# Feed-forward of a two-block model: where VectorE squares a unit's sums, and where the high and low copies of the features are made

## The reference, cut to what matters

```python
for l in range(DEPTH):                                   # DEPTH = 2
    ...
    x = layer_norm(DEEPNORM_ALPHA * x + h, ln1_g[l], ln1_b[l]).astype(dtype)
    f = jnp.square(jax.nn.relu(jnp.einsum('btd,df->btf', x, w_ff1[l])))
    h = jnp.einsum('btf,fd->btd', f, w_ff2[l])
    x = layer_norm(DEEPNORM_ALPHA * x + h, ln2_g[l], ln2_b[l]).astype(dtype)
```

## Time and profile before

| | |
|---|---|
| median of 3 runs | 3498.74 us (3498.04 to 3498.79) |
| the profiled execution | 3498.18 us |
| its span, first instruction to last | 3496.4 us |
| PE busy (matmuls) | 3399.0 us, 97% |
| TensorE's wait in unit 4 for low copies of features | 12.9 us in 8 waits |
| DVE busy | 2225.9 us, 64% |
| ACT busy | 1640.3 us, 47% |
| DMA queue of SP | 56.9% of 16 engines' span |

### The profile page before, as it was taken

One profiled execution on the slowest core, in us unless ns is written; L12 is line 12 of the kernel. 1 busy time (PEld: TensorE's weight loads), 2 busy tenths in 40 slices (PEclk: granted clock), 3 DMA queues, 4 the chain that ended last, 5 costly groups with the idle time before them and its releaser, 6 DMA issues.

```text
span 3496.4 us, 42741 instructions
## 1 busy us (share of the span) xinstructions
PE 3399.0 (97%) x15987; PEld 2831.0 (81%) x15987; DVE 2225.9 (64%) x2582; ACT 1640.3 (47%) x2086; POOL 383.8 (11%) x454
## 2 busy tenths in 40 slices
PE   9999999999999998989999999999999989999999
PEld 7788778888887787878788888878888879888877
DVE  6986565555555688865665555666446776655654
ACT  4444444444444346443544444444445643355553
POOL 0034001010101000340101010100000132000100
PEclk9999999999999999999999999999999999999999
DMA  7655566666666665456666666666666701665634
GB/s 240 178 145 163 181 207 202 197 204 198 203 198 196 185 199 156 139 156 193 241 204 201 201 200 203 200 186 207 186 180 172 209 14 51 188 188 172 177 120 162
DMA packets 326492, 629.63 MB, mean 180 GB/s; under 512 B 25497, under 2 KB 29593, under 8 KB 324651
## 3 DMA queue, kind: packets, MB, share of 16 engines
q1 hardware_dynamic: 313104, 595.93, 56.9%
q0 software_dynamic: 13216, 31.28, 2.8%
HBM read 612.44 MB, written 2.10 MB: 176 GB/s over the span
## 4 chain that ended last, share of the span: by engine, by line
PE 83%; DVE 9%; ACT 3%; DMA 2%; issue 1%; POOL 1%; SPq 1%; DVEq 0%; ACTq 0%; POOLq 0%
PE ps_unit L278 25%; PE ps_unit L280 25%; PE ps_unit L279 25%; DVE sb_w_lo L262 3%; PE ps_mix L2724 2%; DVE sb_conv_y L1252 2%; DMA sb_raw<-in_w_ff_dram 2%; PE ps_mix L1326 1%; ACT sb_w_hi L255 1%; DMA sb_raw<-in_w_in_dram 1%; SPq L875 1%; PE ps_mix L707 0%; PE ps_mix L306 0%; DVE sb_x L437 0%; PE ps_mix L3121 0%
## 5 line engine op out<-in xcount | busy, mean ns | idle before, releaser
L262 DVE TENSOR_TENSOR sb_w_lo<-sb_raw,sb_w_hi 128x1024 fp32r<-128x1024 f32 x1120 | 1381.6, 1248 | 998.1 <-ACT sb_w_hi L255 992.9
L255 ACT ACTIVATE sb_w_hi<-sb_raw 128x1024 fp32r<-128x1024 f32 x1120 | 1173.3, 1059 | 1341.8 <-DMA sb_raw<-in_w_ff_dram 629.7
L278 PE MATMUL ps_unit<-sb_w_hi,sb_a_hi 128*128 128x512 f32 x3456 | 1363.8, 395 | 16.5 <-DVE sb_a_lo L749 11.2
L280 PE MATMUL ps_unit<-sb_w_hi,sb_a_lo 128*128 128x512 f32 x3456 | 1350.4, 391 | 0.0
L279 PE MATMUL ps_unit<-sb_w_lo,sb_a_hi 128*128 128x512 f32 x3456 | 1349.9, 391 | 0.0
L278 PEld LDWEIGHTS ps_unit<-sb_w_hi,sb_a_hi 128*128 128x128 f32 x3456 | 652.0, 189 | 154.9 <-DVE sb_a_lo L749 12.9
L280 PEld LDWEIGHTS ps_unit<-sb_w_hi,sb_a_lo 128*128 128x128 f32 x3456 | 651.5, 189 | 137.7
L279 PEld LDWEIGHTS ps_unit<-sb_w_lo,sb_a_hi 128*128 128x128 f32 x3456 | 652.2, 189 | 132.1
L278 PE MATMUL ps_unit<-sb_w_hi,sb_f_hi 128*128 128x512 f32 x1024 | 401.6, 392 | 12.9 <-DVE sb_f_lo L1005 12.9
L279 PE MATMUL ps_unit<-sb_w_lo,sb_f_hi 128*128 128x512 f32 x1024 | 399.8, 390 | 0.0
L280 PE MATMUL ps_unit<-sb_w_hi,sb_f_lo 128*128 128x512 f32 x1024 | 399.6, 390 | 0.0
(11 more groups left out here) (464 smaller groups left out, 2003.2 us busy)
## 6 DMA issues: line engine op xcount, KB each, us to landing
sb_raw<-in_w_ff_dram SPq DMA_DIRECT2D x512, 512.0 KB, 3.9
sb_raw<-in_w_in_dram SPq DMA_DIRECT2D x224, 512.0 KB, 3.7
sb_raw<-in_e_w_in_dram SPq DMA_DIRECT2D x112, 512.0 KB, 3.6
sb_raw<-in_o_w_in_dram SPq DMA_DIRECT2D x112, 512.0 KB, 3.9
sb_raw<-in_w_out_dram SPq DMA_DIRECT2D x64, 512.0 KB, 4.7
sb_raw<-in_e_w_out_dram SPq DMA_DIRECT2D x32, 512.0 KB, 4.6
sb_raw<-in_o_w_out_dram SPq DMA_DIRECT2D x32, 512.0 KB, 3.7
sb_f_in<-sb_f_out POOLq DMA_DIRECT2D x256, 32.0 KB, 2.0
```

The costliest lines, as they stand in the source:

```text
L255: k.nc.scalar.activation(k.w_hi[:, j], k.raw[:, j], ACT.Copy).then_inc(k.hi_ready, 1)
L262: k.nc.vector.tensor_tensor(k.w_lo[:, j], k.raw[:, j], k.w_hi[:, j].bitcast(F32), ALU.subtract).then_inc(k.lo_ready, 1)
L278: k.nc.tensor.matmul(acc, hi[:, kt, tokens], w_hi, start=kt == 0, stop=False)
L280: last = k.nc.tensor.matmul(acc, lo[:, kt, tokens], w_hi, start=False, stop=kt == KT - 1)
```

## The change

It touches only the loops of the feed-forward part, in the loops of units 1 to 4. VectorE's squaring stood behind split 3 and now stands behind split 1. ACT's high copies stood behind split 4 and now stand behind split 1. VectorE's low copies stood behind split 4 and now stand behind split 2. No instruction is added or taken away, and no wait.

```diff
@@ act_feed_forward, group(): for j in range(AHEAD, AHEAD + 4)
                 act_split(act, k, b0, u * BLOCKS + j)
                 if between:
                     between(u, j - AHEAD)
+                if 1 <= u <= 4 and j == AHEAD + 1:
+                    act.wait_ge(k.relu2_ready, n + u)
+                    for t in range(TT):
+                        last = k.nc.scalar.activation(feature_tokens(k.f_hi, u - 1, t), feature_rows(k, u - 1, t), ACT.Copy)
+                    last.then_inc(k.f_hi_ready, 1)
@@ act_feed_forward, group(): for j in range(AHEAD + 4, AHEAD + 8)
-                if 1 <= u <= 4 and j == AHEAD + 4:
-                    act.wait_ge(k.relu2_ready, n + u)
...
-                    last.then_inc(k.f_hi_ready, 1)
@@ dve_feed_forward, group(): for j in range(AHEAD, AHEAD + 4)
                 dve_split(dve, k, b0, u * BLOCKS + j)
                 if between:
                     between(u, j - AHEAD)
-            if 1 <= u <= 4:
-                dve.wait_ge(k.f_moved_sp[(u - 1) % 2], q * (32 * SP_SQUARES) + (2 * layer * FF_GROUPS + (u + 1) // 2) * 16 * SP_SQUARES)
...
+                if 1 <= u <= 4 and j == AHEAD + 1:
+                    dve.wait_ge(k.f_moved_sp[(u - 1) % 2], q * (32 * SP_SQUARES) + (2 * layer * FF_GROUPS + (u + 1) // 2) * 16 * SP_SQUARES)
+                    dve.wait_ge(k.f_moved_pool[(u - 1) % 2], q * (32 * (SQUARES - SP_SQUARES)) + (2 * layer * FF_GROUPS + (u + 1) // 2) * 16 * (SQUARES - SP_SQUARES))
+                    dve.wait_ge(k.f_kept, n + u)
+                    sums = k.f_in[:, (u - 1) % 2, :]
+                    k.nc.vector.scalar_tensor_tensor(k.f_out[:, (u - 1) % 2, :], sums, 0.0, sums, ALU.max, ALU.mult)\
+                        .then_inc(k.relu2_ready, 1)
+                if 1 <= u <= 4 and j == AHEAD + 2:
+                    dve.wait_ge(k.f_hi_ready, n + u)
+                    for t in range(TT):
+                        last = k.nc.vector.tensor_tensor(feature_tokens(k.f_lo, u - 1, t), feature_rows(k, u - 1, t),
+                                                         feature_tokens(k.f_hi, u - 1, t).bitcast(F32), ALU.subtract)
+                    last.then_inc(k.f_lo_ready, 1)
@@ dve_feed_forward, group(): for j in range(AHEAD + 4, AHEAD + 8)
-                if 1 <= u <= 4 and j == AHEAD + 4:
-                    dve.wait_ge(k.f_hi_ready, n + u)
...
-                    last.then_inc(k.f_lo_ready, 1)
```

More of the change, by code:

```diff
@@ L934, in group @@
                     between(u, j - AHEAD)
-                if 1 <= u <= 4 and j == AHEAD + 4:
-                    act.wait_ge(k.relu2_ready, n + u)
-                    for t in range(TT):
-                        last = k.nc.scalar.activation(feature_tokens(k.f_hi, u - 1, t), feature_rows(k, u - 1, t), ACT.Copy)
-                    last.then_inc(k.f_hi_ready, 1)
             if u < 4:
@@ L1001, in group @@
                     between(u, j - AHEAD)
-                if 1 <= u <= 4 and j == AHEAD + 4:
-                    dve.wait_ge(k.f_hi_ready, n + u)
-                    for t in range(TT):
-                        last = k.nc.vector.tensor_tensor(feature_tokens(k.f_lo, u - 1, t), feature_rows(k, u - 1, t),
-                                                         feature_tokens(k.f_hi, u - 1, t).bitcast(F32), ALU.subtract)
-                    last.then_inc(k.f_lo_ready, 1)
             if u < 4:
```

## The result

The changed kernel takes 3511.49 us (median of 6 runs, 3507.65 to 3512.83), the kernel before 3496.76 us (6 runs, 3493.22 to 3498.79). The ratio is 1.0042, with a 95% interval of 1.0029 to 1.0055: the change makes the kernel slower by 14.7 us. The profiled execution took 3511.99 us with a span of 3510.2, against 3498.18 and 3496.4 before.

A forecast was written before the change was run, and what follows sets the result against it. TensorE, busy 97% of the span, was taken as the bound, so only its waits counted. Group terms summed to +9.6 us on 3498.18, giving 3507.8, with the median 3508 us; own range 3505.7 to 3518, 8-in-10 range 3495 to 3518.

The forecast's parts named there:

- the sum: Feed-forward groups of both layers: gains and losses in TensorE's waits and low clock added up to +9.6 us.
- The likeliest case: Whole kernel: slower than before, chance 0.61; point forecast 3508 us, 0.27% slower.
- more than the sum: Rival: s = 9.0 everywhere and low clock twice as long behind waits of 4 to 5 us; 3516; no separate chance.
- The chain of 5.81: VectorE and ACT, from squaring to the end of the low copies: 5.81 us instead of 3.73.
- A lag is no longer made up: Successive units' transposes on VectorE: with s = 8.8 the period is 21.6 us against TensorE's 21.8; 19.5 before.
- lag: Time from TensorE's end of a unit to the end of its transposes; taken as 2.1 to 9.9 us.
- s: Time from the end of a unit's transposes to the last moved square's landing; 8.8 us where a lag stands, bounds 8.0 and 9.0.
- VectorE and ACT stand still: Both engines idle until the squares land, with seven and more instructions behind the wait; VectorE's idle time 1 to 2 us.
- Group by group: Feed-forward, shift in TensorE's waits and low clock per group: from -2.2 us to +8.3 us in layer 1 group 0.
- The mis-sized term: TensorE behind long waits: each stretch at 1.2 GHz instead of 2.4 costs 1.7 us.
- faster: Rival: s of 8.2 or less where lags stand, so lags are made up; 3493, or 3485 with s = 7.1; chance 0.10.
- Among SP's loads: POOL's last of eight squares, issued 3.75 us behind the transposes among SP's loads of weights, lands after 5.1 us.

The follow-up runs named there:

- the kernel with the shorter chain: Changed kernel with ACT's high copies behind its third split (split 2) instead of its second: 3482.30 us, ratio 0.9959 to the kernel before.

## Why the prediction was right, point by point

*Direction and size.* 3508 us was forecast and 3511.5 measured; on the profiled execution +9.6 was the sum and +13.8 is measured. The likeliest case came true, and near its rival *more than the sum*. That it came out as near as it did is partly luck: the changed groups lost 6.3 us more than the sum had (15.9 against 9.6), and the rest of the program gave 2.1 of it back, most of that by its low clock.

*The chain of 5.81* is 5.83. *A lag is no longer made up*: the period of 21.6 is 21.7 in layer 1 group 0, and in the kernel with the shorter chain the period is 20.2 and VectorE makes up half of its lag. The first period of the groups 0, with ACT's scalings in it, was forecast at 22.4 and was 21.7: with s at 8.5 it came to s + 13.2, not s + 13.6. *VectorE and ACT stand still*: right, but VectorE's idle time in front of the squaring is 2.2 to 4.5 us, not 1 to 2. I had left out that VectorE finishes split 1 before the squares' last part is under way. That idle time is part of s and changes no term.

*Group by group*, forecast and measured: layer 0 groups 1 and 2 -2.2 and -2.0; group 3 -2.1 and -2.8, with the full clock as said; layer 1 group 0 +8.3 and +8.7, with its wait for `sb_w_lo` 1.93 (forecast 1.6), next to none at unit 3 (0.6), 0.86 at block 0 (1.1) and 5.22 at block 6 (5.4); layer 1 group 3 +2.5 and +3.7, its wait 4.76 (4.9). Group 0 of layer 0 was forecast +3.6 and came to +5.8: its wait was 4.85 instead of 3.9, since unit 0 brought in a lag of 7.1 us in this execution instead of the 5.5 of before (5.5 to 7.1 in the six kernels with the bulk loads and the four squares of before), and its low clock cost 3.4 instead of 1.7. Layer 1 groups 1 and 2, -0.5 forecast, came to +2.5. In group 1 unit 3 met a lag of 3.0 and s = 9.2, where I had taken "lags near 2": a wait of 1.84, and a low clock behind it.

*The mis-sized term* is the low clock behind the long waits. I took 1.7 us for each stretch from the earlier trace rows, whose waits were 2.4 to 2.6; behind those of 4.76 to 5.22 it cost 3.2 to 3.4. With the stretch of layer 1 group 1, which the sum did not have, that is 11.7 - 3.4 = +8.3, where the sum had +1.7. The waits went up by 9.3, where it had 7.9. The two misses, 6.6 and 1.4, are more than the 4.2 that are missing, because the rest of the program took 2.1 less, and the groups each came out a little under their two parts.

*s* was taken as 8.8 where a lag stands; in the trace after it is 8.4 to 9.4 there. The rival *faster* needed 8.2 or less, and the runs with 6 squares on SP show that it was the right thing to ask: at s = 5.0 the order of this change wins 12 us. The Trainium skill ("DMA: Bandwidth & Descriptors", "Latency and other measured facts") has about 2 us as a DMA's fixed cost, and the median over all squares is 2.0 in both traces; by it alone s would have been 5.8 and the change a gain. What decided was when the last square is issued and lands, not the usual one. The estimate by that rule, 18 us faster, was thus wrong for this kernel and nearer for the one whose s is 5.0.

*Among SP's loads*: the prediction had POOL's last square land among them, and the issue times bear it out, for the last three of the eight.

*Not settled*: why 3.3 us of lag stay in the groups 0 without the bulk loads, where the other groups have 2, and what makes POOL pause.

## What to carry to other kernels

When a step is moved up to meet its data sooner, follow the whole chain behind it across the engines: here 3.3 us were won in front and 2.1 lost behind, because one engine's copy now stood ahead of the split that the other engine needed for its next step. An in-order engine that waits for a transfer has its slack in front of the wait; ask whether its period with the wait in it is still shorter than that of the engine it feeds, since otherwise no lag it brings in is ever made up. And move both partners' steps by the same place: one number on ACT made the difference between 15 us lost and 13 us won.

## What the runs showed of the hardware

- **How long the low clock lasts can't be told from the wait alone.** In the traces before and after, stretches that cost 1.7 us (1.2 instead of 2.4 GHz over some 3.4 us) stood behind waits of 1.8 to 2.6 us, those that cost 3.2 to 3.4 us behind waits near 5. But 1.84 us had one and 2.10 had none. In the kernel before with 6 squares on SP, 3.31 us had none and 3.12 us cost 3.4. In the kernel before with the later loads, the clock was low for some 10.2 us around the wait of 8.04, of which 4.3 lay in the wait itself, where they cost nothing. And in the changed kernel with the later loads, 4.82 us was followed by the short stretch and 4.66 by the long one:

```profile
1778.00:1782.00 4.00, 3.49 (x9) 2.77 (x10) 2.73 (x3) 0.88 (x1) 0.00 (x0) 0.57 1.02 422
2307.00:2315.00 8.00, 6.59 (x17) 5.25 (x18) 8.00 (x11) 2.96 (x4) 0.00 (x0) 0.57 0.02 7
```

- **How squares are shared out between two queues** moves the last landing by several us: in the changed order s is 10.0 to 11.8 (2 on SP, 10 on POOL; both groups 0 and layer 1 group 3), 7.8 to 9.6 (4 and 8), 5.0 to 6.1 (6 and 6, all units but one). Yet the median time from issue to landing is 2.0 both at 4 and at 6: what decides is how many squares go out behind the first 512 KB load of weights, since those took 3.7 to 4.8 us in the median, and the others 1.7 to 2.0 (one just ahead of the load 2.7).
- **Bulk loads on one queue slow down the other's loads:** weights that SP issued right behind POOL's bulk loads took 5.9 to 14.6 us to land in the changed kernel, and 3.6 to 4.0 with the bulk loads moved away.
- **POOL can pause between two DMA issues** that have nothing to wait for, and at the same place of its program each time: 2.23 us in the three kernels with later loads (which raised s to 12.2 in the one above), 2.62 us in the three with 6 squares on SP.
